# A two-model chain on one core: ScalarE takes the gate tiles out of their PSUM banks

## The chip, the cores and the metric

The kernel runs on one core of one Trainium2 chip, as one launch. The metric is device time in microseconds (us), the median over runs. The engines are TensorE (PE; its weight loads are the rows PEld), VectorE (DVE), ScalarE (ACT), GpSimd (POOL) and SyncE (SP, which issues most DMAs). Each runs its own instruction stream in order, and they meet only at semaphores.

## The reference, cut to what matters

Two models run one behind the other on the same 512 x 1024 activation. The first (a stick-breaking attention layer, an HGRN2 layer, two MLPs) is not touched. The second has two layers; each is

```python
proj = h @ w_in[l]                         # 1024 -> 3600 columns
gq, gk, gv, glr, gz, dq, dk, dv, dz = split_columns(proj)
gqkv = silu(causal_depthwise_conv(concatenate([gq, gk, gv]), conv_w[l]))
o_gla  = gla_branch(gq, gk, gv, glr, ...)  # ends in ... * silu(gz)
o_diff = diff_branch(dq, dk, dv, ...)      # ends in ... * silu(dz)
x = x + gate * (concatenate([o_gla, o_diff]) @ w_out[l])
```

The gated linear attention (GLA) has 4 heads, the differential attention (diff) 4 heads. gz and dz are the gates: 512 columns each, so 4 + 4 tiles of 128 columns in a layer, 16 in the whole second model. This document calls them **z tiles**.

## The kernel before, in words

Everything is kept transposed: 128 features on the partitions, 512 positions along the free axis. A weight tile is 1024 x 128. It comes in as float32 (`raw`), ScalarE rounds it to `w_hi` (`split_hi`, L205), GpSimd takes the rest `w_lo` in four pieces (`split_lo`, L212), and TensorE makes one product tile of 24 matmuls: `w_hi` by `h_hi` (L225), `w_hi` by `h_lo` (L229), `w_lo` by `h_hi` (L232). The product stands in one of two PSUM banks, `ps_g[0]` and `ps_g[1]`, in turn. So tile t+2 can start only when the last reader of tile t's bank is done; the function `reader` names the semaphore for that.

In the second model each layer's order is one list, STEPS, and every engine walks through it and picks out its own part. A tile is two halves of 12 matmuls; behind each half stand the steps that are due there. The items of a layer are GLA pair 0, GLA pair 1 (six tiles each: q, k, v, v, z, z, as c = 0 to 5) and diff heads 0 to 3 (four tiles each: q, k, v, z, as c = 0 to 3). While the tiles of one item are made, the "back" of the item before it is worked off. Counted from 0 in a layer, tile 0 holds the decay gate's input, the z tiles are 5, 6 (GLA pair 0), 11, 12 (GLA pair 1), 16, 20, 24, 28 (diff heads), and the last eight (29 to 36) are the output projection.

A silu is made of five steps, since the exp-and-ln pair is all that ScalarE's table is used for: an absolute value (VectorE, L248, `dve_abs`), exp and ln on ScalarE (L428, L430, step "ln"), a minimum-and-subtract on VectorE (L434, `dve_min`, step "evac2"), exp on ScalarE (L1522, step "exp"), and a product with the source on VectorE (L1575, step "evac3"). One buffer, `bls_b`, serves all of them, so the next absolute value waits for the last minimum. The tiles q, k, v of GLA first go through a four-tap convolution ("taps"): ScalarE makes the first tap out of the bank (L1515), VectorE the other three (L1601), and their silu works on that SBUF copy. For a z tile the source is the PSUM bank itself: L248, L434 and L1575 all read `ps_g`, and the bank is free only behind L1575.

The steps around the z tiles, word for word in the order of the list (c is the tile, G0 and D0 name the item):

- tile 5, second half: evac2(3 G0), evac(4 G0)
- tile 6, first half: exp(3 G0), evac3(3 G0), ln(4 G0), evac2(4 G0), exp(4 G0); second half: evac3(4 G0), evac(5 G0)
- tile 7, first half: ln(5 G0), evac2(5 G0), exp(5 G0), evac3(5 G0), gate(1), decay(G0); second half: gate2(1), taps(0 G1), evac(0 G1), decay2(G0)
- tile 11: first half ends in update(G0), second half: evac2(3 G1), evac(4 G1)
- tile 12: first half: exp(3), evac3(3), ln(4), evac2(4), exp(4), read(G0), square(0 G0); second half: evac3(4), evac(5), stat(0 G0), square(1 G0)
- tile 13: first half: ln(5), evac2(5), exp(5), evac3(5), olo(0 G0), decay(G1); second half: stat(1 G0), evac(0 D0), decay2(G1), turn(0 G1)
- tile 14, first half: olo(1 G0), stat(q D0), turn(1 G1)
- tile 16, second half: evac(3 D0), stat(0 G1), square(1 G1); tile 17: first half: ln(3 D0), evac2(3 D0), exp(3 D0), olo(0 G1), scores(0 D0); second half: evac3(3 D0), ...
- tile 28, second half: evac(3 D3), attn(3 D2), split; then ln(3), evac2(3), exp(3), pv(D2), square(o D2), scores(0 D3), ...

"gemm" of tile k, first half, carries ScalarE's `split_hi` and GpSimd's `split_lo` of tile k+1, and ScalarE's waits for the end of tile k-1. "gate" (L1415 on PE, L1508 on ACT, then an absolute value and L428, L430) and "gate2" (minimum, eight scans L1591) make the decay of a GLA pair. "update" is the chunk recurrence on VectorE (L1653, L1656), "read" the product with the states (L1464), "square" ScalarE's square (L371), "stat" the column sum on PE (L1427), then L385 and L388 on ScalarE, L1627 and L1631 (or L1620 for q and k) on VectorE and L1550 on ScalarE. "decay" is a subtraction on GpSimd (L1706) and two exps on ScalarE (L1553, L1555). "scores" is L1474 on PE, a row maximum on VectorE and the softmax exp on ScalarE (L1566); "attn" turns the result (L1482 on PE, L1689 on VectorE) for "pv" (L1488).

Of the kernel before, what the change touches and what calls it, by code (L numbers as in the profile page):

```python
# [108 lines left out]
def build_program(nc, stream, ada_w, x_in, vecs_in, mats_in, lvmask_in, wgk_in, y_out):  # L109
    with ExitStack() as ctx:  # L110
# [66 lines left out]
        def ev(name):  # L177
            if name not in s:
                s[name] = sem(name)
            return s[name]  # L180

        def vec(name, k=0):
            return vecs[:, VC[name] + k:VC[name] + k + 1]
# [1139 lines left out]
        STATS = [s[1:] for s in STEPS if s[0] == "stat"]  # L1323
        TURNS = [s[1:] for s in STEPS if s[0] == "turn"]
        SWISH = [s[1:] for s in STEPS if s[0] == "evac3"]
        SILUS = [s if s[0] == "gate" else s[1:] for s in STEPS if s[0] == "gate" or s[1:] in SWISH and s[0] == "evac"]

        def nth(order, key, l):
# [3 lines left out]
        def swish_n(c, it, l):  # L1332

            return l * len(SWISH) + SWISH.index((c, it)) + 1

# [4 lines left out]
        def parity(it):  # L1340
            return ITEMS.index(it) % 2
# [9 lines left out]
        b_ls, b_turn = LogSig("b_ls", bls_b), Turn("b_turn", ps_t)  # L1351
        b_unit = Unit("b_unit", M_HEADS, DH, bsq_b, brstd_b)
        cv_first = ev("cv_first")
        bstd_used, bexp_ready, bres_ready, cv_done, dv_ready = (ev("bstd_used"), ev("bexp_ready"), ev("bres_ready"),
                                                                ev("cv_done"), ev("dv_ready"))
        glr_ready, gate_ready, gx_ready, gb_ready = ev("glr_ready"), ev("gate_ready"), ev("gx_ready"), ev("gb_ready")
# [14 lines left out]
        def reader(tile, l):  # L1371

            if tile == 0:
                return glr_ready, l + 1
            if tile < FIRST_TILE["diff", 0]:
                p, c = divmod(tile - 1, 6)
                if c < 4:
                    return cv_done, (l * GLA_PAIRS + p) * 12 + 3 * c + 3
                return bres_ready, swish_n(c, ("gla", p), l)
            h, c = divmod(tile - FIRST_TILE["diff", 0], 4)  # L1380
            if c < 2:
                return bstd_used, nth(STATS, ("qk"[c], ("diff", h)), l).v + 1
            if c == 2:
                return dv_ready, item_n(("diff", h), l) + 1
            return bres_ready, swish_n(c, ("diff", h), l)

        def stat_src(name, it, l):

# [5 lines left out]
        def conv_tile(c, it):  # L1394

            return {0: it[1], 1: 2 + it[1], 2: 4 + 2 * it[1], 3: 5 + 2 * it[1]}[c]

        def silu_src(c, it, l):
            return cv_b[c % 2] if it[0] == "gla" and c < 4 else ps_g[(T_B2 + l * B2_TILES + FIRST_TILE[it] + c) % 2][:]


        def b2_pe(pe, l):
# [90 lines left out]
        def b2_act(act, l):  # L1493
            T = T_B2 + l * B2_TILES
            for s in STEPS:
# [14 lines left out]
                elif s[0] == "taps":  # L1510
                    c = s[1]
                    act.wait_ge(tile_used, T + FIRST_TILE[it] + c + 1)
                    if swish_n(c, it, l) > 2:
                        act.wait_ge(bres_ready, swish_n(c, it, l) - 2)
                    act.activation(cv_b[c % 2], ps_g[(T + FIRST_TILE[it] + c) % 2][:], ACT.Copy,  # L1515
                                   scale=vec(f"conv{l}", 3 * KT + conv_tile(c, it))).then_inc(cv_first, 1)
                elif s[0] == "ln":
                    b_ls.act(act, nth(SILUS, s[1:], l))
                elif s[0] == "exp":
# [57 lines left out]
        def b2_dve(dve, l):  # L1577
            T = T_B2 + l * B2_TILES
            for s in STEPS:
# [13 lines left out]
                elif s[0] == "taps":  # L1593
# [4 lines left out]
                    for tap in range(1, 4):  # L1598
                        if tap > 1:
# [1 line left out]
                        nc.vector.scalar_tensor_tensor(src[:, tap:SEQ], bank[:, 0:SEQ - tap],  # L1601
                                                       vec(f"conv{l}", (3 - tap) * KT + conv_tile(c, it)),
                                                       src[:, tap:SEQ], ALU.mult, ALU.add).then_inc(cv_done, 1)
                elif s[0] == "evac" and (it[0] == "gla" or s[1] == 3):
                    c = s[1]
                    dve.wait_ge(tile_used, T + FIRST_TILE[it] + c + 1)
                    if it[0] == "gla" and c < 4:
                        dve.wait_ge(cv_done, (l * GLA_PAIRS + it[1]) * 12 + 3 * c + 3)
                    b_ls.dve_abs(dve, nth(SILUS, (c, it), l), silu_src(c, it, l))
                elif s[0] == "evac2":  # L1610
                    b_ls.dve_min(dve, nth(SILUS, s[1:], l), silu_src(s[1], it, l), res[parity(it)][s[1]])
                elif s[0] == "evac3":
                    b2_silu_dve(dve, l, s[1], it, silu_src(s[1], it, l))
# [313 lines left out]
```

## Time and profile before

| | us |
|---|---|
| three runs | 1979.60, 1980.22, 1981.69 |
| median | 1980.22 |
| the profiled execution | 1984.43 |
| its span, first to last instruction | 1982.6 |
| second model in it (from about) | 1371 to 1982.6 |

The mean granted TensorE clock of the profiled execution is 0.978. A row of the trace has a start in us from the span's first instruction, a duration, the engine, the line, what it writes and reads, and, in brackets, how long the engine had been idle in front of it and on whom it had waited. Ends of matmuls are modelled, so a run of matmuls is best read by starts: 12 of them start over about 2.7 us at the full clock. Idle time of an engine that is not the limit costs nothing.

### The profile page before, as it was taken

The page shows a single profiled execution, that of the slowest core. Times are in us where ns is not written, and L with a number is a line of the kernel's source. Part 1 is how long each engine was busy: PE and PEld are TensorE (multiplying, and loading weights), DVE is VectorE, ACT ScalarE, POOL GpSimd, SP SyncE. Part 2 cuts the span into 40 slices and gives each one's busy share as a digit, 9 for nine tenths or more (in the row PEclk, how much of TensorE's full clock was granted, in tenths as well). Part 3 has the DMA queues.
Part 4 walks back from the last instruction along what each step waited for, and adds up shares of the span by engine and source line. Part 5 has one row for each costly group of instructions (what it writes and reads, how often), then busy time and mean ns, then how long its engine had stood idle before and what let it go on. Part 6 is the DMA issues. An engine that isn't in the chain of part 4 may idle for free.

```text
span 1982.6 us, 26578 instructions
## 1 busy us (share of the span) xinstructions
PE 1867.1 (94%) x8662; PEld 1460.0 (74%) x8662; DVE 1091.7 (55%) x1691; ACT 879.5 (44%) x1385; POOL 996.1 (50%) x1224
## 2 busy tenths in 40 slices
PE   7999989999999999999899999998999988999988
PEld 5666667887888788888788888886776656776756
DVE  5666647712753467676567317724665553674561
ACT  6667633311433455555343213323554533554441
POOL 3223256655766567677466555654543325443323
PEclk9999989999999999999899999998999988999999
DMA  4211124433443212112144334432221212221212
GB/s 150 64 54 53 53 64 149 159 95 106 164 131 97 85 55 74 54 53 64 43 142 157 106 107 146 153 96 80 75 75 54 64 43 85 64 75 56 72 43 74
DMA packets 49228, 175.32 MB, mean 88 GB/s; under 512 B 5472, under 2 KB 5600, under 8 KB 49136
## 3 DMA queue, kind: packets, MB, share of 16 engines
q1 hardware_dynamic: 42224, 148.98, 24.2%
q10 hardware_dynamic: 6912, 25.17, 3.7%
q8 instruction: 51, 0.84, 0.2%
q14 instruction: 41, 0.34, 0.1%
HBM read 172.03 MB, written 2.10 MB: 88 GB/s over the span
## 4 chain that ended last, share of the span: by engine, by line
PE 76%; DVE 10%; ACT 7%; issue 5%; POOL 1%; DMA 0%; DVEq 0%; ACTq 0%; SPq 0%; POOLq 0%
PE ps_g L225 22%; PE ps_g L229 21%; PE ps_g L232 21%; PE ps_zt L934 2%; PE ps_s L1427 1%; PE ps_o L1488 1%; PE ps_o L962 1%; ACT w_hi L205 1%; PE ps_o L486 1%; DVE scr L1601 1%; PE ps_zt L476 1%; PE ps_s L377 1%; DVE scr L1120 1%; PE ps_zt L468 1%; DVE scr L434 1%
## 5 line engine op out<-in xcount | busy, mean ns | idle before, releaser
L212 POOL TENSOR_TENSOR w_lo<-raw,w_hi 128x256 fp32r<-128x256 f32 x1096 | 898.0, 850 | 916.5 <-ACT w_hi L205 916.5
L205 ACT ACTIVATE w_hi<-raw 128x1024 fp32r<-128x1024 f32 x274 | 289.2, 1056 | 387.0 <-PE ps_g L232 381.6
L225 PE MATMUL ps_g<-h_hi,w_hi 128*128 128x512 f32 x1424 | 411.9, 417 | 32.8 <-ACT h_hi L286 12.0
L229 PE MATMUL ps_g<-h_lo,w_hi 128*128 128x512 f32 x1424 | 379.4, 395 | 0.8 <-DVE h_lo L258 0.8
L232 PE MATMUL ps_g<-h_hi,w_lo 128*128 128x512 f32 x1424 | 375.2, 393 | 0.5 <-POOL w_lo L212 0.2
L225 PEld LDWEIGHTS ps_g<-h_hi,w_hi 128*128 128x128 f32 x1424 | 256.1, 191 | 116.5 <-issue 53.6
L229 PEld LDWEIGHTS ps_g<-h_lo,w_hi 128*128 128x128 f32 x1424 | 271.5, 191 | 62.8 <-DVE h_lo L258 2.1
L232 PEld LDWEIGHTS ps_g<-h_hi,w_lo 128*128 128x128 f32 x1424 | 269.4, 190 | 60.6 <-POOL w_lo L212 3.4
L225 PE MATMUL ps_g<-a_hi,w_hi 128*128 128x512 f32 x768 | 206.1, 405 | 16.3 <-DVE a_lo L1635 7.5
L229 PE MATMUL ps_g<-a_lo,w_hi 128*128 128x512 f32 x768 | 197.8, 393 | 0.0
L232 PE MATMUL ps_g<-a_hi,w_lo 128*128 128x512 f32 x768 | 197.7, 393 | 0.0
L225 PEld LDWEIGHTS ps_g<-a_hi,w_hi 128*128 128x128 f32 x768 | 145.3, 192 | 56.5 <-issue 22.9
L321 DVE TENSOR_TENSOR scr<-ps_g,scr 128x512 f32<-128x512 f32 x32 | 22.1, 692 | 271.5 <-PE ps_g L232 271.5
L232 PEld LDWEIGHTS ps_g<-a_hi,w_lo 128*128 128x128 f32 x768 | 145.3, 189 | 31.9 <-POOL w_lo L212 0.6
L229 PEld LDWEIGHTS ps_g<-a_lo,w_hi 128*128 128x128 f32 x768 | 145.3, 189 | 31.8 <-issue 0.7
L816 ACT ACTIVATE scr<-ps_g 128x512 f32<-128x512 f32 x64 | 38.3, 599 | 211.6 <-PE ps_g L232 211.6
L756 DVE TENSOR_TENSOR scr<-scr,small 128x1024 f32<-128x1024 f32 x48 | 71.3, 1486 | 51.9 <-DMA scr<-ada_weights 51.6
L761 DVE TENSOR_REDUCE scr<-scr 128x128 f32<-128x1024 f32 x48 | 97.3, 2026 | 4.8
L934 PEld LDWEIGHTS ps_zt<-scr 128*128 128x128 f32 x512 | 66.2, 195 | 11.5 <-issue 3.3
L934 PE MATMUL ps_zt<-scr 128*128 128x64 f32 (+1 forms) x512 | 65.2, 274 | 4.6 <-ACT scr L1023 2.1
L858 DVE TENSOR_TENSOR scr<-scr 128x512 f32<-128x512 f32 x64 | 54.9, 858 | 19.3 <-ACT scr L816 18.5
L862 DVE TENSOR_TENSOR a_lo<-scr,a_hi 128x512 f32 (+1 forms) x64 | 58.8, 919 | 10.5 <-DVE scr L858 6.6
(168 smaller groups left out, 2021.0 us busy)
## 6 DMA issues: line engine op xcount, KB each, us to landing
raw<-weights SPq DMA_DIRECT2D x274, 512.0 KB, 3.5
scr<-ada_weights ACTq DMA_DIRECT2D x48, 512.0 KB, 4.3
x<-x_tiles SPq DMA_DIRECT2D x8, 256.0 KB, 5.1
y<-x SPq DMA_DIRECT2D x8, 256.0 KB, 3.3
lvmask<-level_masks SPq DMA_DIRECT2D x1, 512.0 KB, 8.3
mats<-squares SPq DMA_DIRECT2D x1, 448.0 KB, 6.3
vecs<-vectors SPq DMA_DIRECT2D x1, 95.5 KB, 2.0
wgk<-gate_weights SPq DMA_DIRECT2D x1, 32.0 KB, 8.6
```

Of the source, the lines that this page charges most:

```text
L205: nc.scalar.activation(w_hi[:, t.rep % 2], raw[:, raw_slot(t)], ACT.Copy).then_inc(whi_ready, 1)
L212: ins = nc.gpsimd.tensor_tensor(w_lo[:, t.rep % 2, ks], raw[:, raw_slot(t), ks], w_hi[:, t.rep % 2, ks].bitcast(F32), ALU.subtract)
L225: nc.tensor.matmul(bank[:], w_hi[:, t.rep % 2, kk], rhs(k)[0], start=(first and n == 0), stop=False)
L229: nc.tensor.matmul(bank[:], w_hi[:, t.rep % 2, kk], rhs(k)[1], start=False, stop=False)
L232: ins = nc.tensor.matmul(bank[:], w_lo[:, t.rep % 2, kk], rhs(k)[0], start=False, stop=(last and n == len(kts) - 1))
L321: nc.vector.tensor_tensor(tmp_x[0], bank, rstd_x, ALU.mult).then_inc(scaled, 1)
L756: nc.vector.tensor_tensor(ada_b[slot], ada_b[slot], csil.unsqueeze(2).to_broadcast([P, KT, P]), ALU.mult).then_inc(ada_mul, 1)
L761: nc.vector.tensor_reduce(ada_sum[:, slot], ada_b[slot].rearrange("p k f -> p f k"), AX.X, ALU.add).then_inc(ada_part, 1)
L816: act.activation(r_b[k % 2], ps_g[k % 2][:], ACT.Relu).then_inc(relu_done, 1)
L858: nc.vector.tensor_tensor(s_b[k % 2], r_b[k % 2], r_b[k % 2], ALU.mult).then_inc(asq_ready, 1)
L862: nc.vector.tensor_tensor(lo[:, at], s_b[k % 2], hi[:, at].bitcast(F32), ALU.subtract).then_inc(a_ready, 1)
L934: ins = nc.tensor.matmul(out, k[:, ts], rhs, start=True, stop=True)
```

## The change

Each z tile gets an SBUF copy of its own: `z_b`, two 128 x 512 buffers in turn (slots 14 and 15 of `scr2`, which nothing else in the second model uses). In the step "evac" ScalarE waits for the tile and copies the bank into `z_b`; in the step "ln" ScalarE takes the absolute value of the copy, in front of its exp and ln. VectorE's absolute value of the z tiles goes; its minimum and its product read the copy. The bank is free behind the copy (`z_out`). The convolved tiles and the decay gate keep VectorE's absolute value.

```diff
+        Z_TILES = [s[1:] for s in STEPS if s[0] == "evac" and s[1] == (3 if s[2][0] == "diff" else max(s[1], 4))]
...
+        z_b, z_out = [scr2[:, 14], scr2[:, 15]], ev("z_out")
...
@@ def reader(tile, l)
-                return bres_ready, swish_n(c, ("gla", p), l)
+                return z_out, nth(Z_TILES, (c, ("gla", p)), l).v + 1
...
-            return bres_ready, swish_n(c, ("diff", h), l)
+            return z_out, nth(Z_TILES, (c, ("diff", h)), l).v + 1
...
         def silu_src(c, it, l):
-            return cv_b[c % 2] if it[0] == "gla" and c < 4 else ps_g[(T_B2 + l * B2_TILES + FIRST_TILE[it] + c) % 2][:]
+            return z_b[Z_TILES.index((c, it)) % 2] if (c, it) in Z_TILES else cv_b[c % 2]
...
@@ def b2_act(act, l)
+                elif s[0] == "evac" and s[1:] in Z_TILES:
+                    c, n = s[1], nth(Z_TILES, s[1:], l)
+                    act.wait_ge(tile_used, T + FIRST_TILE[it] + c + 1)
+                    if n.v >= 2:
+                        last = Z_TILES[(n.v - 2) % len(Z_TILES)]
+                        act.wait_ge(bres_ready, swish_n(*last, (n.v - 2) // len(Z_TILES)))
+                    act.activation(z_b[Z_TILES.index(s[1:]) % 2], ps_g[(T + FIRST_TILE[it] + c) % 2][:],
+                                   ACT.Copy).then_inc(z_out, 1)
+                elif s[0] == "ln" and s[1:] in Z_TILES:
+                    n, k = nth(Z_TILES, s[1:], l), nth(SILUS, s[1:], l)
+                    act.wait_ge(z_out, n.v + 1)
+                    act.wait_ge(b_ls.ready, k.v)
+                    act.activation(bls_b, z_b[Z_TILES.index(s[1:]) % 2], ACT.Abs).then_inc(b_ls.abs_ready, 1)
+                    b_ls.act(act, k)
...
@@ def b2_dve(dve, l)
-                elif s[0] == "evac" and (it[0] == "gla" or s[1] == 3):
+                elif s[0] == "evac" and it[0] == "gla" and s[1] < 4:
                     c = s[1]
-                    dve.wait_ge(tile_used, T + FIRST_TILE[it] + c + 1)
-                    if it[0] == "gla" and c < 4:
-                        dve.wait_ge(cv_done, (l * GLA_PAIRS + it[1]) * 12 + 3 * c + 3)
+                    dve.wait_ge(cv_done, (l * GLA_PAIRS + it[1]) * 12 + 3 * c + 3)
                     b_ls.dve_abs(dve, nth(SILUS, (c, it), l), silu_src(c, it, l))
                 elif s[0] == "evac2":
+                    if s[1:] in Z_TILES:
+                        dve.wait_ge(z_out, nth(Z_TILES, s[1:], l).v + 1)
                     b_ls.dve_min(dve, nth(SILUS, s[1:], l), silu_src(s[1], it, l), res[parity(it)][s[1]])
```

## Rows read from the trace of the kernel before

**Rows 1.** The page's first part: busy us, share of the span, instructions.

```profile
PE 1867.1 (94%) x8662; PEld 1460.0 (74%) x8662; DVE 1091.7 (55%) x1691; ACT 879.5 (44%) x1385; POOL 996.1 (50%) x1224
```

**Rows 2.** TensorE's waits, 1370 to 1983 us: us in total, times, longest.

```profile
PE ps_zt L1474 <- ACT scr L1566: 10.7, 5, 2.6
PE ps_g L225 <- DVE scr L1575: 7.8, 6, 1.7
...
PE ps_s L1427 <- ACT scr L371: 6.4, 6, 2.2
```

**Rows 3.** Instructions by form, 1370 to 1983 us: busy us, mean ns, idle before.

```profile
L205 ACT ACTIVATE w_hi<-raw 128x1024 fp32r<-128x1024 f32 x70 | 73.8, 1054 | 68.0 <-PE ps_g L232 68.0
...
L1533 ACT ACTIVATE scr<-ps_g 128x512 f32<-128x512 f32 x8 | 4.7, 591 | 5.3 <-PE ps_g L232 5.3
...
L1575 DVE SCALAR_TENSOR_TENSOR scr<-scr 128x512 f32<-128x512 f32 x16 | 18.6, 1160 | 0.0
...
L434 DVE SCALAR_TENSOR_TENSOR scr<-scr 128x512 f32<-128x512 f32 x19 | 13.7, 723 | 4.5 <-ACT scr L430 4.5
...
L1575 DVE SCALAR_TENSOR_TENSOR scr<-scr,ps_g 128x512 f32<-128x512 f32 x16 | 10.9, 684 | 5.6 <-ACT scr L1522 5.6
```

**Rows 4.** The same view over the whole span: ScalarE's absolute value in the first model.

```profile
L1030 ACT ACTIVATE scr<-scr 128x512 f32<-128x512 f32 x24 | 15.0, 624 | 9.7 <-DVE scr L1101 9.7
```

**Rows 5.** In order of time, layer 0, z tiles 5 and 6 and behind them.

```profile
1420.06 0.64 ACT L430 ACTIVATE scr<-scr 128x512 f32<-128x512 f32 x1
...
1425.81 1.17 PE L225 MATMUL ps_g<-h_hi,w_hi 128*128 128x512 f32 x4 [1.60 <-DVE scr L1575]
...
1429.90 0.69 ACT L1508 ACTIVATE scr<-ps_zt,vecs 128x512 f32<-128x512 f32 x1 [0.91 <-PE ps_zt L1415]
...
1434.62 2.29 DVE L1601 SCALAR_TENSOR_TENSOR scr<-ps_g,vecs,scr 128x511 f32<-128x511 f32 x3
...
1438.58 1.07 PE L225 MATMUL ps_g<-h_hi,w_hi 128*128 128x512 f32 x4
...
1445.50 2.32 DVE L1601 SCALAR_TENSOR_TENSOR scr<-ps_g,vecs,scr 128x511 f32<-128x511 f32 x3 [0.22 <-ACT scr L1515]
```

**Rows 6.** In order of time, layer 0, z tiles 11 and 12 and behind them.

```profile
1456.56 2.65 DVE L1656 SCALAR_TENSOR_TENSOR scr<-scr,sml,ps_zt 128x128 f32<-128x128 f32 x7
...
1459.94 0.32 PE L1464 MATMUL ps_o<-scr 64*128 64x64 f32 x1
...
1463.23 0.58 ACT L371 ACTIVATE scr<-ps_o 128x512 f32<-128x512 f32 x1
...
1464.73 1.02 PE L1427 MATMUL ps_s<-scr,mats 128*128 128x512 f32 x2
...
1474.18 1.17 PE L225 MATMUL ps_g<-h_hi,w_hi 128*128 128x512 f32 x4 [1.65 <-DVE scr L1575]
...
1474.65 0.63 ACT L1553 ACTIVATE scr<-scr 128x512 f32<-128x512 f32 x1 [1.33 <-POOL scr L1706]
...
1479.34 1.12 PE L1427 MATMUL ps_s<-scr,mats 128*128 128x512 f32 x2 [2.15 <-ACT scr L371]
```

**Rows 7.** TensorE's waits in the diff part, in order of time, layers 0 and 1.

```profile
1513.47 2.05 PE L225 MATMUL ps_g<-h_hi,w_hi 128*128 128x512 f32 x4 [0.40 <-DVE scr L1575]
...
1604.39 2.42 PE L1488 MATMUL ps_o<-scr 128*128 128x512 f32 x8 [0.94 <-DVE scr L1689]
...
1626.79 0.63 PE L1482 MATMUL ps_zt<-mats,scr 128*128 128x128 f32 x4 [3.33 <-DVE scr L1689]
...
1817.45 1.18 PE L225 MATMUL ps_g<-h_hi,w_hi 128*128 128x512 f32 x4 [0.93 <-DVE scr L1575]
```

**Rows 8.** Stretches: length, busy us of PE, PEld, DVE, ACT, POOL, PEclk, DMA, GB/s.

```profile
1481.00:1486.00 5.00, 5.00 (x20) 3.98 (x20) 1.63 (x3) 1.54 (x4) 2.10 (x4) 0.70 0.35 93
1786.00:1791.00 5.00, 5.00 (x28) 4.17 (x26) 2.04 (x3) 2.87 (x4) 2.81 (x5) 1.00 0.23 52
1627.00:1632.00 5.00, 4.22 (x10) 2.25 (x9) 0.69 (x1) 0.00 (x0) 0.00 (x0) 0.53 0.00 0
```

## The prediction

> **What bounds the kernel now.** I began with the busy shares: TensorE is busy 94% of the span, VectorE 55%, GpSimd 50%, ScalarE 44% [rows 1], so only what makes TensorE wait, or lets its clock fall, can count. The second view is TensorE's waits in the second model. What the change aims at is one line: it stood 7.8 us for VectorE's last product on a z tile, in six waits of at most 1.7 us [rows 2]. The other two lines there are waits for ScalarE: 10.7 us for a softmax exp, 6.4 us for a square. The change gives work to ScalarE, so these matter as much. Third, the rows in order of time around each wait, to see what comes behind it.
>
> They show that the GLA part is bound twice. From tile 7 on, a tile costs TensorE 24 matmuls and some transposes, about 5.8 us. The loop of the convolved tiles costs the same: taps on VectorE, minimum, absolute value, exp and ln on ScalarE, then the first tap of the next tile. VectorE stood only 0.22 us ahead of its taps, for ScalarE [rows 5]. So a delay of this loop, once in, isn't worked off before the convolved tiles end. TensorE runs ahead of it by the slack that two banks give: the last tap of tile 7 ended at 1434.62 + 2.29 = 1436.9, and tile 9, which wants that bank, began at 1438.58 [rows 5]. That is 1.7 us of slack.
>
> **The sum, part by part.** Durations: a copy out of a bank 0.59 (0.5 to the next start), a weight split 1.05, a product or minimum on VectorE 0.69 to 1.2 [rows 3], an absolute value on ScalarE 0.62 [rows 4]; an exp or ln is 0.64 [rows 5], 0.65 from start to start. A semaphore hop is a few hundredths.
>
> *Removed.* 16 absolute values on VectorE; their time falls into idle time except where I follow it below. Six bank waits: 1.60 and 1.65 us are shown for layer 0 [rows 5, 6], then 0.40, and 0.93 at its like in layer 1 [rows 7]; the other two of the six are layer 1's likes of the first two. With a copy the banks are free early enough everywhere: tile 5's at about 1421.2 (behind the ln at 1420.06, plus the copy), wanted at 1425.81 - 1.60 = 1424.2 [rows 5].
>
> *Added, z tiles 5 and 6.* Behind ln at 1420.06 ScalarE has, with nothing to rest on but VectorE's two minima: copy 0.5, split 1.05, exp 0.65, then absolute value, exp, ln, the wait for the minimum and exp (four times 0.65 and 0.75 = 3.35), copy 0.5, split 1.05, and 3.35 again. That is 10.45 us from 1420.65 to 1431.1, where the decay gate's turn comes. Before, it came at 1429.90, after 0.91 us idle [rows 5], so it is 1.2 us late. VectorE does the product on tile 6 just then, in front of the gate's absolute value, and it now reads two SBUF tensors: 1160 ns for such a product against 684 with one in PSUM [rows 3]. So the gate, its scans and the taps of tile 7 come 1.2 to 1.7 us late; I take 1.5, as GpSimd, busy with `w_lo` and the decay, will be there. The taps then end at 1438.4 and tile 9 starts at about 1438.5: where it started before. The 1.60 us are gained at tile 7 and are gone at tile 9, and ScalarE and VectorE are 1.5 us behind.
>
> *Tiles 11 and 12.* The state update ended at 1456.56 + 2.65 = 1459.2, now 1460.7; the read behind it began at 1459.94 [rows 6], now 1460.75: TensorE waits 0.8. ScalarE's square came at 1463.23; now it is 1.5 late and stands behind one absolute value more (0.65), so it ends near 1465.95, and the sum on TensorE that needs it moves from 1464.73 [rows 6] to 1465.9: 1.15 us late. The copy of tile 12 hides under that sum. From here the chain goes by ScalarE (L385, L388, L1550, square, split), GpSimd (`w_lo`, decay), ScalarE's decay exp at 1474.65 and on to the square for which TensorE waited 2.15 us at 1479.34 [rows 6]. The second absolute value lies beside GpSimd's 3.9 us of `w_lo` and decay (ScalarE's own way is 3.3) and costs nothing; if that cover were gone, 0.65. The bank wait of 1.65 lies inside the same stretch: without it TensorE only comes earlier to the wait for the square. So that sum starts at 1480.5: **+1.15 us in each layer, +2.3**.
>
> *Tile 16.* The copy falls into idle time of ScalarE. The absolute value (0.65) does not: the softmax exp of scores(0) is behind it, and TensorE waited up to 2.6 us for such exps [rows 2]. Against it stand the bank waits, 0.40 and 0.93 [rows 7]: +0.25 and -0.28, about 0. *Tiles 20 and 24* have over 1 us of idle ScalarE between exp and square: 0. *Tile 28*: the turned scores leave VectorE before, not behind, an absolute value; of the 0.94 us that pv waited [rows 7] some 0.17 go, since the turn on TensorE itself ended only then: -0.34 for both layers. The copy and absolute value there run beside pv.
>
> *The clock.* This is the term without a row of its own. After the waits of 1.65 and 2.15 us the granted clock was 0.70 over the next 5 us in layer 0 (levels 1 and a half, so 3 us at half speed, 1.5 us lost), and 1.00 at the same place in layer 1 [rows 8]. Behind a single wait of 3.33 us [rows 7] it was 0.53 [rows 8]. The change turns the two waits into one of about 3.8 us (tile 14 starts at 1473.7, its half is done at 1476.7, the square comes at 1480.5). So I expect the fall in layer 1 as well: +1.5. The bounds are 0 (as layer 1 was) and +3 (one fall more in each layer); below 0 to -1.5 if layer 0's fall goes.
>
> Sum: 2.3 - 0.03 - 0.34 + 1.5 = **+3.4 us**. On the profiled execution, 1984.43, which is 4.2 us above the median of the runs, that gives 1987.8; on the median 1980.22 it gives **1983.6**.
>
> *A rule against the change.* Products with two SBUF inputs took 1160 ns on average and 684 with one input in PSUM, while minima with two SBUF inputs took 723 [rows 3]. The Trainium skill, "GPSIMD Engine Reference", section "Key points", says that GpSimd shares its SBUF interfaces with VectorE, with contention for VectorE instructions that have two SBUF inputs. By it every z tile's minimum and product are exposed, by the rows mainly the product. Its consequence, as a mechanism of this kernel, is the second rival.
>
> **The rivals.** *The whole gain.* If ScalarE had room, the 7.8 us would go and nothing would come: 1972.4. For it: ScalarE is the least busy engine [rows 1]. Against it: that share is an average; between 1420 and 1431 it has no idle time left but the minima. *More contention (slower).* Each z tile's minimum costs 1.2 instead of 0.7 when GpSimd works. Two such minima stand between 1420 and 1431, one more before the square, so 1.5 us per layer beyond my sum: 1983.6 + 3 = 1986.6. It decides when GpSimd's `w_lo` of tiles 7, 8 and 13 overlaps these minima; that minima of convolved tiles average 723 beside the same GpSimd work speaks against it. *The clock stays.* As forecast, but no fall in layer 1: 1982.1. Two places that did differ before show that it is not settled by the waits alone. *The change doesn't do what it says*, as the copy is queued behind ScalarE's ln: the bank is free late. It is so at tile 5, by 2 us, and still in time; it would cost nothing beyond the sum.
>
> **How the numbers follow.** About 0.2% (4 us) is what a measurement of this kernel can tell from no change: below 1976.3 is faster, above 1984.2 slower. My forecast 0.45, clock stays 0.22, more contention 0.18, whole gain 0.08, and 0.07 for chains that I mis-walked, both ways. The forecast is only 0.6 us under the bound of slower, so I give four tenths of it to slower; with contention that makes 0.43 slower, 0.46 same, 0.11 faster. The range leaves out the whole gain and goes from 1978.0 (delay of 1.2 instead of 1.5, and a fall of the clock gone in layer 0) to 1988.0 (contention and one more fall).
>
> **What would show it.** TensorE's waits for L1575 are gone. Tile 9 starts about where it did, with a wait for the taps in front. There is a new wait ahead of L1464 (0.8) and a short one ahead of the first L1427 sum, and the one at 1479 grows from 2.15 to some 3.8 us. Products on z tiles take 0.7 to 1.2. The prediction is wrong if tile 9 starts over a microsecond earlier than 1438.6, if there is no wait ahead of the read, or if minima go over 1 us.

## The result, and the profile after

The changed kernel takes **1990.49 us** (median of 5 runs, 1988.89 to 1991.88) against 1981.02 for the kernel before (5 runs, 1979.6 to 1984.83). The ratio is 1.0042, 95% interval 1.0029 to 1.0056: slower, by 9.5 us by the medians. A second set (6 runs against 17) gave 1.0048, 1.0031 to 1.0066.

The profiled execution of after took 1989.19 us (span 1987.4, mean granted clock 0.975), only 4.8 us more than that of before: the execution of before was 3.4 us above its median, that of after 1.3 below. Of these 4.7 us, 2.6 lie in the first model, which the change doesn't touch. A place that shows this is the first matmul of the decay gate in the second model (L1415 before, L1417 after):

```profile
1392.95 1.12 PE L1415 MATMUL ps_zt<-scr,wgk 16*128 16x512 f32 x2
```

and in the kernel after:

```profile
1390.31 1.12 PE L1417 MATMUL ps_zt<-scr,wgk 16*128 16x512 f32 x2
```

From there to the end of the span it is 1982.6 - 1392.95 = 589.7 us before and 1987.4 - 1390.31 = 597.1 after: **+7.4 us in the second model**. Over all kernels below this start moves between 1387.2 and 1394.1, so from here on "second model" means this stretch, and it scatters less than the whole (the changed kernel's second profile gave 595.7). Line numbers of after are 2 to 16 higher than before: L1427 is L1429, L1464 is L1466, L1474 is L1476, L1566 is L1582, L1575 is L1591, L1601 is L1617, L1656 is L1672, L1706 is L1722.

The busy shares of after, where [rows 1] had those of before:

```profile
PE 1870.1 (94%) x8662; PEld 1459.7 (73%) x8662; DVE 1085.8 (55%) x1675; ACT 894.8 (45%) x1417; POOL 993.9 (50%) x1224
```

32 instructions more on ScalarE, 16 fewer on VectorE, and nothing that explains 7 us. TensorE's waits in the second model do (us in total, times, longest; before in [rows 2]):

```profile
PE ps_zt L1476 <- ACT scr L1582: 11.8, 4, 3.8
PE ps_s L1429 <- ACT scr L371: 11.6, 8, 4.5
...
PE ps_g L225 <- DVE scr L1617: 3.1, 2, 1.6
...
PE ps_o L1466 <- DVE scr L1672: 1.2, 2, 0.6
```

The 7.8 us for the product are gone. In their place stand 3.1 for the taps and 1.2 for the state update, and the wait for a square went from 6.4 to 11.6. The forms of after (busy us, mean ns, idle before; [rows 3] before):

```profile
L1591 DVE SCALAR_TENSOR_TENSOR scr<-scr 128x512 f32<-128x512 f32 x32 | 32.6, 1020 | 9.5 <-ACT scr L1538 9.5
...
L434 DVE SCALAR_TENSOR_TENSOR scr<-scr 128x512 f32<-128x512 f32 x36 | 27.1, 754 | 45.4 <-ACT scr L430 45.4
...
L1531 ACT ACTIVATE scr<-scr 128x512 f32<-128x512 f32 x16 | 9.9, 619 | 0.0
L1525 ACT ACTIVATE scr<-ps_g 128x512 f32<-128x512 f32 x16 | 9.4, 590 | 27.1 <-PE ps_g L232 27.1
```

Copy and absolute value cost what was forecast (590 and 619 ns). All 36 minima now read two SBUF tensors and average 754; 16 products more do too. (Before it was 20 minima, of 722 on average; [rows 3] counts from about 1400 us and so has 19.) Last, the rows in order of time in layer 0:

```profile
1423.26 0.58 ACT L1525 ACTIVATE scr<-ps_g 128x512 f32<-128x512 f32 x1
...
1428.23 1.46 DVE L1591 SCALAR_TENSOR_TENSOR scr<-scr 128x512 f32<-128x512 f32 x1 [0.70 <-ACT scr L1538]
...
1433.60 2.29 DVE L1617 SCALAR_TENSOR_TENSOR scr<-ps_g,vecs,scr 128x511 f32<-128x511 f32 x3
...
1436.03 1.16 PE L225 MATMUL ps_g<-h_hi,w_hi 128*128 128x512 f32 x4 [1.58 <-DVE scr L1617]
...
1458.17 0.32 PE L1466 MATMUL ps_o<-scr 64*128 64x64 f32 x1 [0.61 <-DVE scr L1672]
...
1463.40 1.12 PE L1429 MATMUL ps_s<-scr,mats 128*128 128x512 f32 x2 [0.28 <-ACT scr L371]
...
1469.60 3.26 POOL L212 TENSOR_TENSOR w_lo<-raw,w_hi 128x256 fp32r<-128x256 f32 x4 [9.44 <-ACT w_hi L205]
1471.47 0.79 DVE L434 SCALAR_TENSOR_TENSOR scr<-scr 128x512 f32<-128x512 f32 x1 [4.05 <-ACT scr L430]
1472.82 1.04 POOL L1722 TENSOR_TENSOR scr<-scr 128x512 f32<-128x512 f32 x1
1472.96 1.45 DVE L1591 SCALAR_TENSOR_TENSOR scr<-scr 128x512 f32<-128x512 f32 x1 [0.70 <-ACT scr L1538]
1473.89 0.63 ACT L1569 ACTIVATE scr<-scr 128x512 f32<-128x512 f32 x1 [0.96 <-POOL scr L1722]
1478.58 2.07 PE L1429 MATMUL ps_s<-scr,mats 128*128 128x512 f32 x2 [4.46 <-ACT scr L371]
...
1510.30 1.21 DVE L1651 TENSOR_TENSOR a_lo<-scr,a_hi 128x512 fp32r<-128x512 f32 x1
...
1513.41 1.22 PE L1476 MATMUL ps_zt<-scr 64*128 64x256 f32 x4 [3.77 <-ACT scr L1582]
```

Counted from the layer's first gate matmul, tile 9 starts 45.72 us in (1436.03 - 1390.31) against 45.63 before: where it did, now behind the taps. The sum on GLA pair 0 ("stat(0)") starts at 73.1 against 71.8. The wait of 2.15 us in [rows 6] is 4.46. The scores of diff head 0 wait 3.77 us for their exp, where it was 2.64 (the longest of that line in [rows 2]); the prediction had 0.65 more there. The piece of `w_lo` ahead of the decay takes 3.26 us; before it was

```profile
1470.83 2.79 POOL L212 TENSOR_TENSOR w_lo<-raw,w_hi 128x256 fp32r<-128x256 f32 x4 [8.60 <-ACT w_hi L205]
```

The clock, in the columns of [rows 8], behind the wait of 4.46 us in either layer:

```profile
1478.00:1485.00 7.00, 6.42 (x16) 4.51 (x17) 2.53 (x4) 2.79 (x5) 2.79 (x4) 0.54 0.22 53
1785.00:1792.00 7.00, 4.66 (x12) 3.15 (x13) 4.07 (x7) 3.38 (x5) 2.78 (x4) 0.53 0.01 2
```

Half speed (1.2 of 2.4 GHz is a granted 0.5) nearly throughout, in both layers; before it was 0.70 and 1.00 [rows 8].

### The profile page after: what moved, and what is told of

Its sections match the earlier page's. It is cut to its first block, busy times and chain, and to the rows that moved or that the text cites. A ratio compares the mean times of both kernels' runs of the same rounds, so it can differ in the third digit from the quotient of the medians.

```text
span 1987.4 us, 26624 instructions
## 1 busy us (share of the span) xinstructions
PE 1870.1 (94%) x8662; PEld 1459.7 (73%) x8662; DVE 1085.8 (55%) x1675; ACT 894.8 (45%) x1417; POOL 993.9 (50%) x1224
## 4 chain that ended last, share of the span: by engine, by line
PE 75%; DVE 10%; ACT 8%; issue 6%; POOL 1%; DMA 0%; DVEq 0%; ACTq 0%; SPq 0%; POOLq 0%
PE ps_g L225 22%; PE ps_g L229 21%; PE ps_g L232 20%; PE ps_zt L934 2%; PE ps_s L1429 1%; PE ps_o L1490 1%; ACT w_hi L205 1%; DVE scr L1617 1%; PE ps_o L962 1%; PE ps_o L486 1%; DVE scr L434 1%; PE ps_zt L476 1%; ACT scr L428 1%; PE ps_zt L1476 1%; PE ps_s L377 1%
## 5 line engine op out<-in xcount | busy, mean ns | idle before, releaser
L434 DVE SCALAR_TENSOR_TENSOR scr<-scr 128x512 f32<-128x512 f32 x60 | 47.6, 794 | 76.9 <-ACT scr L430 74.9
```

Of the source, the lines that this page charges most:

```text
L434: return nc.vector.scalar_tensor_tensor(dst, src, 0.0, self.buf, ALU.min, ALU.subtract).then_inc(self.ready, 1)
```

## The experiments

Theories going in: **ScalarE**: the absolute value and the copy lengthen ScalarE's queue, and TensorE waits for what is queued behind. **Contention**: the product and the minimum, now with two SBUF inputs, collide with GpSimd. **Clock**: the longer waits let the clock fall. Each run is a kernel of its own beside the kernel before on the same chip. The ratio comes from many runs; the last column is one profiled execution, so the two can disagree by some microseconds. The edits below are cut and, where nothing else is said, stand against the changed kernel; the line for the diff tiles in `reader` changes like the one shown for GLA. All numbers first:

| kernel | us (runs) | before | ratio [95%] | second model |
|---|---|---|---|---|
| before | | | | 589.7 |
| changed, again | 1990.99 (6) | 1983.31 | 1.0048 [1.0031, 1.0066] | 595.7 |
| e1 copy, abs on VectorE | 1984.93 (12) | 1982.82 | 1.0017 [1.0006, 1.0029] | 589.9 |
| e2 abs on ScalarE, no copy | 1986.47 (11) | 1982.82 | 1.0019 [1.0008, 1.0030] | 590.2 |
| e3 copy made, not used | 1989.38 (7) | 1982.82 | 1.0034 [1.0020, 1.0048] | 592.6 |
| e8 minimum from the bank | 1984.21 (11) | 1982.82 | 1.0007 [0.9996, 1.0018] | 589.6 |
| e4 GLA z tiles only | 1988.93 (8) | 1983.62 | 1.0032 [1.0019, 1.0044] | 595.6 |
| e5 diff z tiles only | 1982.05 (10) | 1983.62 | 0.9997 [0.9984, 1.0010] | 588.5 |
| e6 changed, filled | 1982.68 (12) | 1983.62 | 1.0002 [0.9991, 1.0012] | 587.6 |
| e7 before, filled | 1977.42 (12) | 1983.62 | 0.9969 [0.9958, 0.9980] | 582.8 |
| e13 minimum from the bank, filled | 1978.97 (12) | 1983.31 | 0.9987 [0.9976, 0.9998] | 584.3 |
| e9 changed, decay first | 1985.18 (12) | 1982.65 | 1.0021 [1.0009, 1.0033] | 589.8 |
| e11 before, decay first | 1978.32 (12) | 1982.65 | 0.9979 [0.9969, 0.9988] | 584.6 |
| e10 before, decay first, filled | 1974.85 (5) | 1982.65 | 0.9961 [0.9948, 0.9974] | 580.4 |
| e12 diff only, decay first, filled | 1977.44 (7) | 1982.65 | 0.9966 [0.9952, 0.9980] | 582.9 |

And the landmarks in layer 1, from the layer's first gate matmul to the start of a sum on TensorE, in us. In the filled kernels (e7, e6, e13) no half speed lies in these stretches, in either layer; in the others it can.

| kernel | stat(0) | first stat, diff head 0 | first stat, diff head 1 |
|---|---|---|---|
| before / changed | 71.7 / 73.1 | 86.4 / 88.3 | 123.3 / 127.4 |
| e1 / e2 / e3 | 72.1 / 72.2 / 72.7 | 87.8 / 86.8 / 87.4 | 125.5 / 124.4 / 125.3 |
| e8 | 72.6 | 87.3 | 124.0 |
| e4 / e5 | 73.1 / 71.7 | 88.3 / 86.3 | 127.3 / 125.1 |
| e7 / e6 / e13 (filled) | 71.7 / 73.1 / 72.6 | 86.3 / 88.2 / 87.3 | 121.7 / 124.4 / 123.0 |
| e11 / e9 | 71.7 / 72.4 | 84.9 / 86.5 | 122.7 / 125.1 |

### One part at a time

**e1**: the copy stays, the absolute value goes back to VectorE (reading the copy).

```diff
 # ACT, step "ln"
-                    act.wait_ge(z_out, n.v + 1)
-                    act.wait_ge(b_ls.ready, k.v)
-                    act.activation(bls_b, z_b[...], ACT.Abs).then_inc(b_ls.abs_ready, 1)
 # DVE
+                elif s[0] == "evac" and s[1:] in Z_TILES:
+                    dve.wait_ge(z_out, nth(Z_TILES, s[1:], l).v + 1)
+                    b_ls.dve_abs(dve, nth(SILUS, s[1:], l), silu_src(s[1], it, l))
```

> Alone: ScalarE copies the z tile, VectorE takes the absolute value of the copy, as it did of the bank; the early release of the bank stays. Theory A (the time is lost on ScalarE, which has the copy and the absolute value in its chain, 0.5 and 0.65 us a tile): the absolute value is the larger part, so 0 to +3 us over the kernel before, and the wait for scores(1) of diff head 0 falls from 3.8 back to about 2.7 us. Rival B (the loss is contention, since minimum and product read two SBUF tensors beside GpSimd): they still do, so +6 us or more. Rival C (the loss is the clock, because the two TensorE waits are merged into one): the waits are still merged at the first stat of diff head 0, so half or more of the +9.5 stays.

**e2**: the absolute value stays on ScalarE, but reads the bank; no copy, all readers on the bank, which is free behind the product as before.

```diff
-                return z_out, nth(Z_TILES, (c, ("gla", p)), l).v + 1
+                return bres_ready, swish_n(c, ("gla", p), l)
 # silu_src of a z tile: the bank; ACT "evac" of z tiles dropped; in "ln":
-                    act.wait_ge(z_out, n.v + 1)
+                    act.wait_ge(tile_used, T + FIRST_TILE[it] + s[1] + 1)
```

> Alone: no copy; ScalarE takes the absolute value out of the bank, minimum and product read the bank, which is freed behind the product, as before the change. Theory A: about 0.85 us of backlog behind each pair of GLA z tiles and 0.65 in front of the scores, +2 to +4 us over the kernel before, with a wait of about 3.3 us for scores(1). Rival B: no operand has moved into SBUF, so no contention: same time as before, within 1 us. Rival C: two TensorE waits stay two, so the half-speed stretches stay as they were before the change.

**e3**: ScalarE does all that the change gives it, but minimum and product read the bank and free it late.

```diff
-                return z_out, nth(Z_TILES, (c, ("gla", p)), l).v + 1
+                return bres_ready, swish_n(c, ("gla", p), l)
-            return z_b[...] if (c, it) in Z_TILES else cv_b[c % 2]
+            return ps_g[(T_B2 + l * B2_TILES + FIRST_TILE[it] + c) % 2][:] if (c, it) in Z_TILES else cv_b[c % 2]
```

> Copy and absolute value on ScalarE as in the changed kernel, but minimum and product read the bank, and the bank is freed only behind the product: ScalarE's load as changed, no early release, no second SBUF operand on VectorE. Theory A: +5 to +8 us over the kernel before (the changed kernel's +9.5 less about 1 us a layer of contention). Rival B: 0 to +2 us. Rival C: the bank waits come back (about 2.5 us each for tiles 7 and 14), the wait at the first stat of diff head 0 is near 2.2 again and the clock falls less.

Measured, in layer 1: the absolute value alone (e2) puts stat(0) and the first stat of diff head 0 0.4 us later each; the copy beside it (e3 against e2) 0.5 and 0.7; the two SBUF operands on top (changed against e3) 0.4 and 0.8, though the banks come free earlier. So three parts of similar size, not one. e1, e2 and e3 are slower than before by 3.4, 3.8 and 6.7 us by their ratios, clear of noise each: e1 a little above what theory A gave it (and its wait for the scores is 3.10, not 2.7), e2 and e3 inside it.

e1 has almost the early release and the contention without the absolute value. Its second model of 589.9 looks like that of before, but that was the fastest of its 12 executions. Its first stat of diff head 0 comes 1.4 us late in layer 1. Its wait at that stat is 4.92 us, longer than the changed kernel's 4.46, with an earlier sum: a wait's length says how early TensorE came, not how late the work was.

**e8**: as changed, but the minimum reads the bank and frees it; only the product reads the copy. This takes most of the contention out and keeps ScalarE's queue.

```diff
-                return z_out, nth(Z_TILES, (c, ("gla", p)), l).v + 1
+                return b_ls.ready, nth(SILUS, (c, ("gla", p)), l).v + 1
-                    b_ls.dve_min(dve, nth(SILUS, s[1:], l), silu_src(s[1], it, l), res[parity(it)][s[1]])
+                    b_ls.dve_min(dve, nth(SILUS, s[1:], l), bank_src(s[1], it, l), res[parity(it)][s[1]])
```

> As the changed kernel, but the minimum reads the bank and frees it; only the product reads the copy. Theory A: same ScalarE load, +7 to +9 us over the kernel before; the split of w_lo beside the minimum takes 2.8 us instead of 3.3 at tile 14, so the stat of diff head 0 comes 0.5 us earlier in each layer. Rival B: the minimum is the contended half; with it gone half of the loss goes, +4 to +5 us.

By the ratio e8 is 1.4 us slower than before, and not clearly; both theories asked for 4 us or more. The second model is 6.1 to 7.5 us shorter than the changed one, of which 2.7 are left once the clock is held (e13 below). The stat of diff head 0 comes 1.0 us earlier, where 0.5 was expected. In order of time, at the place shown above:

```profile
1471.63 2.78 POOL L212 TENSOR_TENSOR w_lo<-raw,w_hi 128x256 fp32r<-128x256 f32 x4 [9.44 <-ACT w_hi L205]
...
1473.49 0.69 DVE L434 SCALAR_TENSOR_TENSOR scr<-ps_g,scr 128x512 f32<-128x512 f32 x1 [4.04 <-ACT scr L430]
```

With the bank as one operand of the minimum, GpSimd's four subtractions take 2.78 again instead of 3.26, and the minimum 0.69 instead of 0.79. The same split takes 2.79 in e2 and 2.78 in e3, where the minimum reads the bank, and 3.26 in e1, where it reads the copy though ScalarE has no absolute value. **It is the minimum's operand that slows this split.** Other VectorE instructions with two SBUF inputs go with the same lengthening: in the kernel before, the split that starts at 1507.29 took 3.24 us, beside a minimum that reads the bank and `a_lo`, the rest that the rounding to `a_hi` leaves, which has two SBUF inputs:

```profile
1507.29 3.24 POOL L212 TENSOR_TENSOR w_lo<-raw,w_hi 128x256 fp32r<-128x256 f32 x4 [9.54 <-ACT w_hi L205]
```

The Trainium skill, "SBUF — State Buffer", section "Who interferes with whom", has a VectorE instruction with two SBUF inputs contend with a GpSimd instruction that reads SBUF, and not one with at most one such input outside its 2-port modes. These four kernels agree, and they show the side that the prediction left out: GpSimd pays too.

Against e3 (same ScalarE work, bank held until the product), e8 differs by nothing at the first stat of diff head 0 in layer 1 (87.3 and 87.4), though e3 has bank waits of 2.57 and 2.41 us there. In that layer the early release, which was the change's aim, buys nothing up to this stat. In layer 0 it does: behind e3's wait at tile 7 the clock fell,

```profile
1426.56 1.17 PE L225 MATMUL ps_g<-h_hi,w_hi 128*128 128x512 f32 x4 [2.59 <-DVE scr L1591]
```

```profile
1428.00:1432.00 4.00, 4.00 (x9) 2.19 (x8) 1.38 (x2) 1.57 (x3) 3.01 (x4) 0.60 0.24 57
```

the gate came late with it, and the first stat of diff head 0 is at 89.1 against 87.3 in e8. The same wait in layer 1 had no fall behind it.

### By place

**e4** and **e5**: the change on the GLA or on the diff z tiles alone; the others keep the old way.

```diff
-        Z_TILES = [s[1:] for s in STEPS if s[0] == "evac" and s[1] == (3 if s[2][0] == "diff" else max(s[1], 4))]
+        Z_TILES = [s[1:] for s in STEPS if s[0] == "evac" and s[2][0] == "gla" and s[1] >= 4]    # e4
+        Z_TILES = [s[1:] for s in STEPS if s[0] == "evac" and s[2][0] == "diff" and s[1] == 3]   # e5
```

> The change on the eight GLA z tiles alone; the diff z tiles keep VectorE's absolute value out of the bank. Theory A (backlog of ScalarE and contention behind tiles 5, 6, 11, 12, plus one merged wait that costs clock): the stat of diff head 0 comes 1.9 us later in each layer, as in the changed kernel, and the wait for scores(1) is back at 2.7; +5 to +7 us over the kernel before. Rival D (the loss is in the diff part): within 2 us of the kernel before.

> The change on the eight diff z tiles alone. Theory A: the scores(1) wait of diff head 0 grows from 2.65 by 1.1 us (0.65 absolute value, 0.5 contention), less the bank waits of 0.40 and 0.93: 0 to +2 us over the kernel before. Rival D: +6 us or more.

By time the GLA z tiles carry the loss (595.6 us of second model; the changed kernel 597.1 and 595.7; 6.3 us by the ratio) and the diff tiles none (588.5 against 589.7; the ratio can't be told from 1). e4 came out as theory A had it. By the landmarks it is not so simple: e5 has the wait of 3.78 us at the scores, against 2.64 in e4, and is 1.8 us late at head 1 in layer 1. Tile 16 does lose. What e5 has for it is clock in layer 0. Behind its stat for diff head 0, and over 10 us at the scores:

```profile
1478.00:1485.00 7.00, 6.17 (x29) 4.83 (x30) 3.47 (x6) 4.59 (x7) 3.03 (x5) 1.00 0.16 37
1510.00:1520.00 10.00, 9.13 (x32) 6.25 (x33) 8.28 (x24) 6.12 (x15) 3.11 (x4) 0.83 0.12 44
```

and the same two stretches of the kernel before:

```profile
1478.00:1485.00 7.00, 5.66 (x18) 4.28 (x19) 3.29 (x6) 3.38 (x5) 2.79 (x4) 0.76 0.11 15
1510.00:1520.00 10.00, 7.75 (x23) 5.12 (x23) 7.60 (x24) 5.67 (x14) 2.67 (x4) 0.66 0.19 53
```

Its waits ahead of the first stretch are those of before, and the clock still differs: a fall of the clock can come and go with shifts that no wait shows, which is why the next kernels hold it.

### The clock held

**e6** and **e7** (and e10, e12, e13): idle matmuls into a bank whose content is overwritten next, ahead of the two long waits of each layer. e6 has 13 and 15 of them, e7 7 and 10, to fit the waits.

```diff
+                    if s[1:] == ("q", ("diff", 0)):
+                        pe.wait_ge(b_unit.ln_done, n.v)
+                        for _ in range(13):
+                            nc.tensor.matmul(ps_s[:], w_hi[:, (T + 14) % 2, 0], h_hi[:, 0], start=True, stop=True)
...
+                    if (j, it) == (1, ("diff", 0)):
+                        pe.wait_ge(b_turn.done, nth(TURNS, ("v", it), l).v + 1)
+                        for _ in range(15):
+                            nc.tensor.matmul(ps_t[:], w_hi[:, (T + 17) % 2, 0], h_hi[:, 0], start=True, stop=True)
```

> The changed kernel, with 13 matmuls of no use ahead of the first stat of diff head 0 and 15 ahead of its scores(1), into banks that are free there (0.23 us each, so 3.0 and 3.4 us inside waits of 4.5 and 3.8 us). Output unchanged. Theory A' (part of the loss is TensorE's clock falling behind these two longer waits): the half-speed stretches at about 1478, 1512, 1785 and 1822 go, and the time falls by 3 to 6 us below the changed kernel. Without clock effects (rival: the loss is queueing alone): no shorter, or longer by up to 1 us.

> The kernel before with the same filling, 7 and 10 matmuls (1.6 and 2.3 us inside waits of 2.15 and 2.65 us). Theory A': the half-speed stretches at 1481, 1511 and 1818 go, 2 to 5 us faster than the kernel before; the difference between the two filled kernels is then what the queues alone cost, about 4 us (2 per layer). Rival (no clock effect): same as the kernel before.

The waits of e6 (line, what it waited for, total, times, longest) and, in the columns of [rows 8], the clock behind the two filled waits in layer 0:

```profile
PE ps_zt L1484 <- ACT scr L1590: 5.9, 5, 2.2
PE ps_s L1433 <- ACT scr L371: 3.6, 8, 0.5
```

```profile
1475.00:1482.00 7.00, 6.92 (x33) 5.14 (x32) 3.08 (x5) 4.20 (x6) 3.41 (x5) 1.00 0.20 63
1510.00:1520.00 10.00, 9.48 (x38) 6.24 (x37) 7.86 (x24) 7.03 (x15) 3.59 (x5) 1.00 0.17 52
```

The granted clock is 1.00 at both, and at their likes in layer 1. Filled, the changed kernel is no slower than the plain kernel before, but the kernel before, filled, is 0.31% faster; both gained more than was expected (8 to 9 us and 6). The change then costs 587.6 - 582.8 = 4.8 us in the second model (5.3 by the medians, 6.5 by the ratios), against 7.4 and 6.0 unfilled. The landmarks are cleaner, since no half speed lies before them: 124.4 - 121.7 = 2.7 us in a layer up to the first stat of diff head 1, **5.4 us for both**, where the unfilled kernels differ by 7.6 and 6.2. So of the loss 1 to 3 us is the clock, and 5 us is queue. Of the 2.7, 1.9 are there at the first stat of diff head 0, and 0.75 come between it and that of head 1, where tile 16 lies.

**e13**: e8 with filling of the same kind (9 and 13).

> The kernel in which the minimum reads the bank and frees it, with 9 and 13 filling matmuls ahead of the stat and scores(1) of diff head 0, so that the clock stays up as in the filled changed kernel. If the gap between the minimum-from-bank kernel and the changed kernel is contention on the way to these two waits, about 1 us per layer is left of it with the clock held: 1.5 to 2.5 us under the filled changed kernel's ratio of 1.0002 (so 0.999), and the rest of the gap was clock. If the gap was clock alone, the same ratio as the filled changed kernel.

At the first stat of diff head 1, e13 lies 1.3 us above e7 and 1.4 below e6 in a layer, 2.6 and 2.7 for both. The ratios agree (3.6 and 3.0). The second models say 1.5 and 3.3 instead, but nothing holds the clock in the part behind this landmark. From it in layer 1 to the end, in e6, e7 and e13:

```profile
1813.94:1974.80 160.86, 145.78 (x604) 104.95 (x604) 74.44 (x198) 66.44 (x129) 53.56 (x72) 0.96 0.20 63
1815.03:1975.60 160.57, 145.42 (x605) 104.33 (x603) 75.60 (x199) 63.07 (x121) 52.26 (x72) 0.96 0.19 63
1815.10:1974.60 159.50, 142.98 (x604) 102.90 (x604) 74.11 (x198) 66.50 (x129) 52.25 (x72) 0.98 0.20 63
```

e13 had a higher clock there and was 1.1 to 1.4 us shorter. Its edit doesn't explain that: unfilled, e8 with the same edit has 161.0 us there and the changed kernel 160.9. So with the clock held **about half of the 5.4 us goes with the minimum's operand** (contention, net of what the slightly later release costs e13), **and about half with ScalarE's longer queue** and what contention the product keeps. No run takes the product's operand out alone.

### The chain behind the split

If the first stat of diff head 0 hangs on GpSimd's split and decay, issuing the decay ahead of that split must move it, in either kernel.

```diff
-                if s[0] == "gemm" and s[2] == 0:
+                if s[0] == "gemm" and s[2] == 0 and s[1] not in (7, 13):
                     split_lo(...)
 # behind the decay's subtraction
+                    split_lo(pool, At(T + {0: 7, 1: 13}[it[1]] + 1))
```

> The changed kernel, with GpSimd's decay subtraction of a GLA pair issued ahead of the split of tiles 8 and 14 instead of behind it. Theory A (the chain to the first stat of diff head 0 goes by that split and decay, 4.3 us behind ScalarE's split; ScalarE's own way there, absolute value, exp, ln, minimum, exp, is about 3.5 us): the wait of 4.5 us at that stat shrinks by 0.8 to 1 us in each layer and the wait stays above 3.3; 1 to 3 us faster than the changed kernel. Rival (ScalarE's own work sets the chain): no change.

> The same move in the kernel before, where ScalarE's own way is only 2.7 us behind its split: the wait of 2.15 us at that stat shrinks by 1.2 to 1.3 us in each layer, 2 to 4 us faster than the kernel before (the half-speed stretch behind it may go too). Rival: no change.

It does: in the kernel before the wait of 2.15 us [rows 6] became

```profile
1478.27 1.12 PE L1427 MATMUL ps_s<-scr,mats 128*128 128x512 f32 x2 [0.71 <-ACT scr L371]
```

and in the changed kernel 4.46 became

```profile
1479.90 2.08 PE L1429 MATMUL ps_s<-scr,mats 128*128 128x512 f32 x2 [3.39 <-ACT scr L371]
```

So the exposed chain runs over GpSimd, as the prediction had it. The second model shortened by 5.1 us (before) and by 6 to 7 (changed), more than the 1.5 and 1.8 per layer that the landmark moved, and more than the 2 to 4 and 1 to 3 us that were expected. Part of the rest is clock: behind that stat, where before has 0.76 above, e11 has

```profile
1478.00:1485.00 7.00, 6.73 (x32) 5.25 (x33) 2.91 (x5) 4.03 (x6) 3.55 (x6) 1.00 0.26 73
```

How large each part is was not split further.

### A version that beats both

**e10** is the kernel before with the decay first and the filling (3 and 10); **e12** adds the change on the diff z tiles (3 and 15).

> The kernel before with the decay moved and with filling matmuls (3 ahead of the stat, 10 ahead of scores(1)). If both effects are real and add: 8 to 10 us below the kernel before (6 of the filling alone, 2 to 3 of the move).

> As the last one, with the change made on the diff z tiles alone (filling 3 and 15). Theory A: the 1.1 us more in front of scores(1) and the bank waits of about 1 us that go cancel once the clock stays up: within 1.5 us of the last one. If the early release of the bank were worth its full wait, 2 us faster than it.

e10 is the fastest of all: 0.39% under the kernel before, 7.7 us where 8 to 10 were expected. e12 is no better. The two ratios' intervals overlap, but at the first stat of diff head 1, with no half speed before it in either kernel, e12 is 0.8 us later in layer 0 and 0.7 in layer 1 (121.1 and 121.0 against 120.3): what tile 16 costs in e6 against e7 as well. The expectation that it and the bank waits cancel was wrong. The changed kernel taken once more, beside the kernel before of e13:

> The changed kernel once more, beside the same runs of the kernel before as the run above: ratio 1.004 with more runs and a narrower interval, and again TensorE waits of 4.4 to 4.5 us and 3.8 us with a half-speed stretch behind each.

The ratio of 1.0048 and the waits (4.47 and 4.46 us, 3.77 twice) came again; the interval did not get narrower.

## Why the prediction was wrong

The direction and the first landmarks were right, the size was not: +3.4 us forecast, +7.4 and +6.0 in the two profiles' second models, +9.5 and +7.7 by the medians. A part of the distance to 1990.49 is the base: the three runs shown had a median of 1980.22, this set 1981.02 and the wider sets 1982.65 to 1983.62, so 1 to 3 us are the starting point, which the prediction had noted (4.2 us between profile and median) and then resolved towards the median. Two steps of the sum failed, of about the same size.

- **Tiles 5 to 9: right.** The bank wait is gone, tile 9 starts 0.1 us later than it did, with 1.58 us of wait for the taps. The convolved loop came 1.6 us late (1433.60 + 2.29 - 1390.31 = 45.58 against 43.96); I took 1.5.
- **The product on tile 6: right in kind, too low.** 1.46 us; the mean of two-SBUF products, 1160 ns, had been taken. The delay at the taps (1.6 for 1.5) held it all the same.
- **The read: right.** 0.61 us, forecast 0.8.
- **stat(0): nearly right.** +1.3 in a layer, forecast 1.15.
- **"The second absolute value lies beside GpSimd's 3.9 us ... and costs nothing": this step failed.** The absolute value itself stayed covered (ScalarE still waited 0.96 us for the decay), but the cover did not keep its length. The minimum on a z tile's copy (0.79 us, at 1471.47), beside the split, stretched `w_lo` from 2.79 to 3.26 us, and this split is in the chain itself. It started 1.4 us late and ended 1.9 late, and the first stat of diff head 0 came 1.9 us late in each layer, where I had carried 1.15: 1.5 us missing for both. I had asked whether a minimum would be slow beside GpSimd and answered with its mean of 723 ns; it was 0.79 here and 754 on average, so that answer held and was the wrong question.
- **Tile 16, "+0.25 and -0.28, about 0": this step failed too.** With the clock held it costs 0.75 us in each layer, 1.5 for both. The wait at the scores was 3.77 us against 2.64 with the old diff tiles (e4): +1.13 us. I had named the absolute value (0.65) in front of the exp: e2, e3 and e8 have a wait of 3.33, so it is 0.69. The other 0.44 is VectorE's part of the chain to the scores. Its minimum took 0.09 more, and its `a_lo`, with two SBUF inputs and not edited at all, took 1.21 us, beside the last of GpSimd's `w_lo` (it ended at 1510.96), and 0.86 in e3 and e8. Before it was

```profile
1509.04 0.91 DVE L1635 TENSOR_TENSOR a_lo<-scr,a_hi 128x512 fp32r<-128x512 f32 x1
```

- **Tile 28: right.** The wait of pv went from 0.94 to 0.78 us in either layer, forecast 0.17 less, and pv itself comes 0.17 sooner behind the one before it. **Tiles 20 and 24: right**, nothing moved there.
- **The clock, +1.5: about right.** Layer 1 fell as forecast (0.53 for 1.00). The filled pair puts the term between 1.2 and 2.6 us by the second models, between 0.9 and 2.2 by the landmarks.

With the clock held, the queue costs 5.4 us up to tile 16 of both layers where the sum had 2.3. The 3.1 missing are the two failed steps. The minimum's operand (2.7) is nearly as large; how the rest falls was not taken apart. The rival "more contention" had the size (+3 us) with the wrong victim: its minima were to take 1.2 us, and the longest in the changed kernel takes 0.86. Slower had 0.43 and same 0.46, from a forecast that lay 0.6 us under the bound: the true sum was well beyond it. These chances don't follow from their own terms either: 0.18 and 0.18 make 0.36 for slower and leave 0.49 for same before the 0.07 is shared out. And the lower end of the range, 1978.0, is 2 us below what its two reasons give (0.6 and 3.0 under 1983.6).

## What to carry to other kernels

What a bank wait is worth is what comes next in the chain: here 6.5 us of it in four places bought nothing in GLA, since the convolved loop and a square were due at the same time. It can still be worth a fall of the clock, as in layer 0 of e3. An edit that moves an operand from PSUM to SBUF on VectorE is an edit of GpSimd's times too: price every GpSimd instruction that lies beside it, above all one that is used as cover. And where a wait can't be removed, idle matmuls through it were worth more than the change under test.

## What the runs showed of the hardware that was not expected

- Filling two waits per layer took 0.31% off the kernel before, and the changed kernel's second model from 597.1 and 595.7 to 587.6 us. The matmuls do no work; the gain is that the matmuls behind the wait run at a granted 1.00 (the first stat of diff head 0 itself comes when it did, at 86.3 and 86.4). Behind the filled wait, at the place where [rows 8] has 0.70, the filled kernel before has:

```profile
1479.00:1486.00 7.00, 6.90 (x32) 5.40 (x33) 2.74 (x5) 3.87 (x6) 3.73 (x6) 1.00 0.25 75
```

- One VectorE instruction of 0.8 us with two SBUF inputs lengthened four GpSimd subtractions beside it by 0.47 us (2.79 to 3.26), and GpSimd's next one, the decay, lengthened the product from 0.69 to 1.45 us.
- Which of the two pays goes with who started first. In the changed kernel the decay had started 0.14 us before the product: it kept its 1.04 us, and VectorE took all of the delay. In e1 the product had started 0.55 us before the decay, and the decay took 1.49:

```profile
1469.39 1.14 DVE L1588 SCALAR_TENSOR_TENSOR scr<-scr 128x512 f32<-128x512 f32 x1 [0.70 <-ACT scr L1535]
1469.94 1.49 POOL L1722 TENSOR_TENSOR scr<-scr 128x512 f32<-128x512 f32 x1
```

- Where VectorE came second, three rows give an estimate of its time: what was left of the decay, and 0.54 us. The product in the changed kernel (0.90 left) took 1.45, the product in e8 at the same place (0.53 left) 1.07, and `a_lo` in the kernel before (0.67 left) 1.21:

```profile
1473.95 1.21 DVE L1635 TENSOR_TENSOR a_lo<-scr,a_hi 128x512 fp32r<-128x512 f32 x1
```
